# All four groups of a visit gathered and scattered by POOL, without tests of the token count

## The chip, the core and the metric

One core of a Trainium2 chip. The metric is the device time of one execution in microseconds (us). The kernel before takes 1515.26 us, the median of three runs (1512.69 to 1515.73). The core has TensorE (PE in the profile, its weight loads PEld), VectorE (DVE), ScalarE (ACT), GpSimd (POOL) and SyncE (SP), and 16 DMA engines that all queues share.

## What is computed

One decoder layer for 512 tokens of width 1024, in float32: a gated DeltaNet group and a convolution group side by side, one output projection, and then a mixture of experts. The last part is where the change lies. Cut to what matters:

```python
def _moe(xn, w_router, b_router, w_gate_up, b_gate_up, w_down, b_down):
    logits = (xt @ w_router + b_router).astype(jnp.float32)
    top_val, top_idx = lax.top_k(logits, TOP_K)          # 4 of 32 experts for each token
    gates = jax.nn.softmax(top_val, axis=-1)
...
    def expert_block(args):
        x_blk, e = args
        hid = x_blk @ w_gate_up[e] + b_gate_up[e]
        gate, up = hid[:, :D_FF], hid[:, D_FF:]
        gate = jnp.minimum(gate, SWIGLU_LIMIT)
        up = jnp.clip(up, -SWIGLU_LIMIT, SWIGLU_LIMIT)
        glu = gate * jax.nn.sigmoid(SWIGLU_ALPHA * gate)
        return ((up + 1.0) * glu) @ w_down[e] + b_down[e]
...
    y = jax.ops.segment_sum(weighted, row_tok, num_segments=t + 1)[:t]
```

512 tokens with 4 experts each are 2048 pairs over 32 experts, 64 for an expert on average.

## The kernel before

The first 420 us or so compute the two mixing groups, the output projection and the router. Then the kernel goes through the experts one after the other, a **visit** each. With the counts of these inputs there are 32 visits. A visit has room for 128 tokens, in four **groups** of 32 slots (`GROUPS`, `GROUP`). A group's tokens lie on 128 partitions: each token's row of 1024 numbers is cut into four quarters, and each quarter has a partition of its own. So a gather or a scatter of one group handles 128 rows of 256 numbers (1 KB). TensorE skips the matmuls of groups 2 and 3 when the visit has no more than 64 or 96 tokens; groups 0 and 1 are always computed.

DVE works out, from the router's choice, for every slot the row in memory (`idx`). A slot without a token gets a number of 2048 or more, past the bound that both indirect transfers are given (`bounds_check=PAST - 1`), and such a row is skipped.

POOL's part is the loop at L605 that this case is about. It runs 31 times (`m` is 30), once for each visit but the last. Pass `i` has two halves:

- The **gather half** waits until TensorE has turned the tokens of visit `i + 1` (`xt_done`), copies the four index columns of visit `i + 2` (`fetch_rows`, L551), and issues the gathers of that visit into `xg` (a part of `wq`; `gather`, L556). They raise `gathered` by 16 each. TensorE waits for that before it turns these tokens, one pass later (`xt_turn`).
- The **scatter half** waits until ACT has written the results of visit `i - 1` into `yb` (a part of `rows`; `y_ready`), copies the indices (L551 again), and issues the scatters, which add to `acc_dram` in memory (`scatter`, L561). They raise `scattered` by 16 each. POOL then waits until all scatters so far have landed and raises `landed`. ACT waits for `landed` before it writes the next visit's results over `yb`, and POOL itself can't begin the next gather half before.

Groups 0 and 1 are issued always. For groups 2 and 3 the helper `full_or_idle` reads the visit's token count from `left` into a register and branches: a group with tokens gets its gather or scatter, one without gets `idle` (L568), a transfer of 16 bytes from `gdn_dt_bias` into the tile `spare`, so that the semaphore rises by 16 all the same. The three visits whose gathers stand ahead of the loop (12 gathers), and the last visit's scatters behind it (4), have no test: all four groups are issued there.

The other queues around it: SP issues a visit's weights, 8 transfers of 1 MB for gate/up into the eight slots of `ring` (L375) and 4 of 1 MB for down into `dslots` (L380), each when TensorE has used the slot before (`gu_used`, `d_used`). TensorE, in pass `i`, runs the gate/up matmuls of visit `i` (L1869), turns the gathered tokens of visit `i + 1` (L1836), and runs the down matmuls of visit `i - 1` (L1905) with the turning of the hidden values between (L1931). ACT copies the hidden values (L887) and writes the results (L895). DVE applies the biases and the gate (L1431 to L1450). At the end SP waits for `scattered`, loads the sum back (L419), and it is normalised and written out.

Of the kernel before, what the change touches and what calls it, by code (L numbers as in the profile page):

```python
# [32 lines left out]
GROUP = 32  # L33
GROUPS = 4
# [4 lines left out]
def block_kernel(nc, x, attn_norm_w, w_in, gdn_conv_w, gdn_a_log, gdn_dt_bias, gdn_norm_w, cf_dw_w, cf_dw_b,  # L39
# [3 lines left out]
    H = gdn_a_log.shape[1]  # L43
# [27 lines left out]
    with ExitStack() as ctx:  # L71
        def sb(name, cols, dt=F32):
            return ctx.enter_context(nc.sbuf_tensor(name, [P, cols], dt))
# [22 lines left out]
        idx_in, idx_out = sb("idx_in", GROUPS, I32), sb("idx_out", GROUPS, I32)  # L96
        n_iter = sb("n_iter", 1, I32)
        left = sb("left", ROUNDS_MAX * E + 2, I32)
        spare = sb("spare", 4 * H)
        count16 = sb("count16", 2 * P, BF16)  # L100
        tri16, ones16 = count16[:, 0:P], count16[:, P:2 * P]

# [227 lines left out]
        def tokens_left(engine, i):  # L330

            return engine.value_load(left[0:1, bass.ds(i, 1)], min_val=0, max_val=SEQ)
# [94 lines left out]
        def _(pool):  # L427
# [135 lines left out]
                                        in_=yb[:, g, :], in_offset=None, bounds_check=PAST - 1,  # L563
                                        oob_is_err=False, compute_op=ALU.add).then_inc(scattered, 16)

            def idle(k, done):

                pool.dma_start(spare[0:1, k * H:(k + 1) * H], gdn_dt_bias[0:1, :]).then_inc(done, 16)  # L568

            def full_or_idle(i, full, empty):  # L570

                tokens = tokens_left(pool, i)
                with pool.If(tokens > 2 * GROUP):
                    full(2)
                    with pool.If(tokens > 3 * GROUP):
                        full(3)
                    with pool.Else():
                        empty(3)
                with pool.Else():
                    empty(2)  # L580
                    empty(3)

            pool.wait_ge(idx_ready, 1)
            fetch_rows(idx_in, 0, 1)
            for g in range(GROUPS):
# [19 lines left out]
            with pool.Fori(1, m + 2) as i:  # L605
                pool.wait_ge(idx_ready, i + 3)
                pool.wait_ge(xt_done, i + 2)
                pool.sem_inc(pool_step, 1)
                fetch_rows(idx_in, (i + 2) % STAGES, i * 2 + 2)
                for g in range(2):  # L610
                    gather(g)
                full_or_idle(i + 2, gather, lambda g: idle(g - 2, gathered))
                pool.wait_ge(y_ready, i + 1)
                pool.sem_inc(pool_step, 1)
                fetch_rows(idx_out, (i - 1) % STAGES, i * 2 + 3)
                for g in range(2):
                    scatter(g)
                full_or_idle(i - 1, scatter, lambda g: idle(g, scattered))
                pool.wait_ge(scattered, i * (16 * GROUPS))
                pool.sem_inc(landed, 1)  # L620
            pool.wait_ge(y_ready, m + 3)
# [1365 lines left out]
```

## Time and profile before

| | |
|---|---|
| median of three runs | 1515.26 us |
| the profiled execution | 1512.43 us |
| its span, first to last instruction | 1510.7 us |
| TensorE busy | 1369.0 us (91%) |
| DVE, ACT, POOL busy | 565.8, 301.8, 368.6 us (37, 20, 24%) |
| DMA | 451.10 MB, mean 299 GB/s; about 400 in the expert stage |
| weights of the experts | 256 + 124 + 4 transfers of 1 MB |
| POOL's loop: gathers, scatters, small transfers | 88, 83, 93 |

How to read it: the busy times are of one profiled execution, so everything that is added up from the trace is held against 1512.43 us; the difference to the 1510.7 us of the span lies outside the first and last instruction. Two engines or an engine and the DMA can be busy at once, so the busy times say only who has room. Who is waited for is told by the views of waits, which name for each idle time what ended it, and by the timeline, which gives an engine's instructions one by one with the idle time before each.

### The profile page before, as it was taken

The page shows a single profiled execution, that of the slowest core. Times are in us where ns is not written, and L with a number is a line of the kernel's source. Part 1 is how long each engine was busy: PE and PEld are TensorE (multiplying, and loading weights), DVE is VectorE, ACT ScalarE, POOL GpSimd, SP SyncE. Part 2 cuts the span into 40 slices and gives each one's busy share as a digit, 9 for nine tenths or more (in the row PEclk, how much of TensorE's full clock was granted, in tenths as well). Part 3 has the DMA queues.
Part 4 walks back from the last instruction along what each step waited for, and adds up shares of the span by engine and source line. Part 5 has one row for each costly group of instructions (what it writes and reads, how often), then busy time and mean ns, then how long its engine had stood idle before and what let it go on. Part 6 is the DMA issues. An engine that isn't in the chain of part 4 may idle for free.

```text
span 1510.7 us, 33686 instructions
## 1 busy us (share of the span) xinstructions
PE 1369.0 (91%) x13162; PEld 633.5 (42%) x13163; DVE 565.8 (37%) x1174; ACT 301.8 (20%) x566; POOL 368.6 (24%) x434
## 2 busy tenths in 40 slices
PE   6997989879899999999999999988988988889982
PEld 3444555555433444343433444433433433334441
DVE  2888888553522223322232212332222223222231
ACT  3122323131301212121211112211111111112122
POOL 4001111010221232331342223232223223222323
PEclk9999999979969999999999999999999999999996
DMA  9211000300387999999999999999999999999974
GB/s 301 79 66 56 1 29 1 148 21 18 125 312 298 375 382 388 399 410 406 408 399 409 405 410 409 405 408 401 401 410 403 407 405 399 399 404 406 401 302 139
DMA packets 109974, 451.10 MB, mean 299 GB/s; under 512 B 18264, under 2 KB 36852, under 8 KB 77142
## 3 DMA queue, kind: packets, MB, share of 16 engines
q1 hardware_dynamic: 86566, 427.88, 70.8%
q0 software_dynamic: 20304, 21.03, 6.1%
q10 hardware_dynamic: 3072, 1.76, 0.5%
q8 instruction: 21, 0.34, 0.1%
q14 instruction: 11, 0.09, 0.0%
HBM read 439.05 MB, written 17.17 MB: 302 GB/s over the span
## 4 chain that ended last, share of the span: by engine, by line
PE 61%; DMA 20%; DVE 10%; SPq 4%; ACT 2%; issue 2%; POOL 0%; ACTq 0%; DVEq 0%; POOLq 0%
PE bank L1869 28%; DMA ring<-in_w_gate_up_dram 19%; PE bank L1905 12%; PE bank L1552 5%; PE bank L1719 4%; PE bank L1931 3%; DVE dslots L1007 2%; SPq L380 2%; SPq L375 2%; PE bank L1836 1%; DVE qkbuf L1031 1%; PE bank L1854 1%; PE bank L1618 1%; PE bank L1547 1%; PE bank L1825 1%
## 5 line engine op out<-in xcount | busy, mean ns | idle before, releaser
L1869 PE MATMUL bank<-ring,wq 128*32 128x512 f32 x5184 | 590.0, 608 | 49.3 <-DMA ring<-in_w_gate_up_dram 46.4
L1869 PEld LDWEIGHTS bank<-ring,wq 128*32 128x32 f32 x5184 | 163.7, 112 | 425.2 <-issue 424.5
L1905 PE MATMUL bank<-dslots,intra 128*32 128x256 f32 x5056 | 286.0, 380 | 0.0
L1905 PEld LDWEIGHTS bank<-dslots,intra 128*32 128x32 f32 x5056 | 157.8, 110 | 108.6 <-issue 11.1
L887 ACT ACTIVATE wq<-bank 128x512 f32<-128x512 f32 x128 | 66.1, 602 | 632.3 <-PE bank L1869 632.3
L561 POOL DMA_INDIRECT acc_rows<-rows,idx_out x83 | 151.0, 1819 | 46.2 <-POOL idx_out L551 28.3
L1431 DVE TENSOR_TENSOR intra<-bank,small 128x256 f32<-128x256 f32 x128 | 45.4, 417 | 293.1 <-PE bank L1931 293.1
L1552 PE MATMUL bank<-hbuf,ring 128*128 128x512 f32 x320 | 147.7, 603 | 0.0
L1360 DVE TENSOR_REDUCE small<-bank 128x4 f32<-128x8 f32 x34 | 5.7, 167 | 343.9 <-PE bank L1825 343.9
L551 POOL COPY idx_in<-idx 128x4 int32 (+1 forms) x34 | 6.3, 186 | 456.9 <-PE bank L1836 405.7
L556 POOL DMA_INDIRECT wq<-xn_rows,idx_in x88 | 91.9, 1044 | 49.7 <-POOL idx_in L551 29.3
L1007 DVE SCALAR_TENSOR_TENSOR dslots<-dslots,small 128x512 f32<-128x512 f32 x120 | 91.8, 765 | 2.7
L1438 DVE TENSOR_TENSOR zrows<-bank,small 128x256 f32<-128x256 f32 x128 | 45.4, 417 | 101.7 <-PE bank L1931 101.7
L1552 PEld LDWEIGHTS bank<-hbuf,ring 128*128 128x128 f32 x320 | 58.7, 194 | 58.4 <-issue 58.4
L1931 PE MATMUL bank<-consts,wq 128*128 128x128 f32 x512 | 70.8, 282 | 2.7 <-DVEq L1434 1.6
L901 ACT ACTIVATE zrows<-intra 128x1024 f32<-128x1024 f32 x32 | 33.8, 1057 | 185.0 <-DVE intra L1435 185.0
L568 POOL DMA_DIRECT2D spare<-in_gdn_dt_bias_dram x93 | 69.3, 848 | 0.1
L1931 PEld LDWEIGHTS bank<-consts,wq 128*128 128x128 f32 x512 | 55.7, 142 | 28.7 <-issue 25.5
L1719 PE MATMUL bank<-ring,dslots 128*128 128x512 f32 x128 | 59.6, 611 | 1.9 <-DVE dslots L1186 1.9
L895 ACT ACTIVATE rows<-bank,small 128x256 f32<-128x256 f32 x128 | 50.2, 475 | 51.6 <-PE bank L1905 51.6
L551 POOL COPY idx_out<-idx 128x4 int32 (+1 forms) x32 | 6.8, 214 | 210.1 <-ACT rows L895 210.1
L1339 DVE TENSOR_SCALAR rows<-slot_no,small 128x512 bf16<-128x512 bf16 x140 | 40.1, 351 | 10.5 <-DVE idx L1363 10.3
(267 smaller groups left out, 1040.6 us busy)
## 6 DMA issues: line engine op xcount, KB each, us to landing
ring<-in_w_gate_up_dram SPq DMA_DIRECT2D x256, 1024.0 KB, 21.3
dslots<-in_w_down_dram SPq DMA_DIRECT2D x124, 1024.0 KB, 24.5
ring<-in_w_in_dram SPq DMA_DIRECT2D x12, 1024.0 KB, 12.1
ring<-in_w_out_dram SPq DMA_DIRECT2D x4, 1024.0 KB, 4.8
ring<-in_w_down_dram SPq DMA_DIRECT2D x4, 1024.0 KB, 20.5
rows<-in_x_dram SPq DMA_DIRECT2D x4, 512.0 KB, 6.6
hbuf<-in_x_dram SPq DMA_DIRECT2D x4, 512.0 KB, 4.6
xn_rows<-convbuf POOLq DMA_DIRECT2D x4, 512.0 KB, 4.2
```

The source lines that it names most:

```text
L556: pool.indirect_dma_start(out=xg[:, g, :], out_offset=None, in_=xn_q, in_offset=bass.IndirectOffsetOnAxis(ap=idx_in[:, g:g + 1], axis=0), ...
L561: pool.indirect_dma_start(out=acc_q, out_offset=bass.IndirectOffsetOnAxis(ap=idx_out[:, g:g + 1], axis=0), in_=yb[:, g, :], in_offset=None ...
L568: pool.dma_start(spare[0:1, k * H:(k + 1) * H], gdn_dt_bias[0:1, :]).then_inc(done, 16)
L887: A(hid[:, g, :], bank[g][:, :], ACT.Copy).then_inc(hid_ready, 1)
L895: ins = A(yb[:, g, :], bank[4 + g // 2][:, (g % 2) * QD:(g % 2 + 1) * QD], ACT.Copy, scale=gates[:, bass.ds(stage * GROUPS + g, 1)])
L1007: own.mark(V.scalar_tensor_tensor(out=cacc[:, j, :], in0=ubuf[:, j, k:k + SEQ], scalar=PT[:, j, k:k + 1], in1=cacc[:, j, :], op0=ALU.mult, ...
L1431: V.tensor_tensor(four(g2[:, g, :, :]), four(src[g]), bias(0), ALU.add).then_inc(s, 1)
L1552: ins = M(bank_of(s)[:, :], unit_ap(u)[:, c, half * P:(half + 1) * P], hT[:, c, :], start=(c == 0), stop=(c == KC - 1))
L1719: ins = M(pair[half][:, :], lhs, w, start=(kc == 0), stop=(kc == KC - 1))
L1869: ins = M(bank[g][GROUP * j:GROUP * (j + 1), :], xT[:, g, c % 2, (c // 2) * GROUP:(c // 2 + 1) * GROUP], w[:, :, j * QD:(j + 1) * QD], sta ...
L1905: ins = M(b[GROUP * j:GROUP * (j + 1), col:col + QD], actT[:, g, c % 2, (c // 2) * GROUP:(c // 2 + 1) * GROUP], w[:, cc, j * QD:(j + 1) * QD],
L1931: ins = TR(bank[6 + g // 2][:, c:c + P], hid[:, g, half * QD + hh * P:half * QD + (hh + 1) * P], ident)
```

## The change

In the loop of POOL, groups 2 and 3 get their gather and their scatter in every pass, like groups 0 and 1. The helpers `idle` and `full_or_idle` go, with the reading of the token count on POOL, its branches, and the tile `spare`. The counts that everyone waits for stay the same, since a gather or scatter raises its semaphore by 16 as the small transfer did. Nothing changes on the other engines: TensorE still tests the count and skips its matmuls.

```diff
--- before.py
+++ after.py
@@ -96,7 +96,6 @@
         idx_in, idx_out = sb("idx_in", GROUPS, I32), sb("idx_out", GROUPS, I32)
         n_iter = sb("n_iter", 1, I32)
         left = sb("left", ROUNDS_MAX * E + 2, I32)
-        spare = sb("spare", 4 * H)
         count16 = sb("count16", 2 * P, BF16)
         tri16, ones16 = count16[:, 0:P], count16[:, P:2 * P]
 
@@ -563,23 +562,6 @@
                                         in_=yb[:, g, :], in_offset=None, bounds_check=PAST - 1,
                                         oob_is_err=False, compute_op=ALU.add).then_inc(scattered, 16)
 
-            def idle(k, done):
-
-                pool.dma_start(spare[0:1, k * H:(k + 1) * H], gdn_dt_bias[0:1, :]).then_inc(done, 16)
-
-            def full_or_idle(i, full, empty):
-
-                tokens = tokens_left(pool, i)
-                with pool.If(tokens > 2 * GROUP):
-                    full(2)
-                    with pool.If(tokens > 3 * GROUP):
-                        full(3)
-                    with pool.Else():
-                        empty(3)
-                with pool.Else():
-                    empty(2)
-                    empty(3)
-
             pool.wait_ge(idx_ready, 1)
             fetch_rows(idx_in, 0, 1)
             for g in range(GROUPS):
@@ -607,15 +589,13 @@
                 pool.wait_ge(xt_done, i + 2)
                 pool.sem_inc(pool_step, 1)
                 fetch_rows(idx_in, (i + 2) % STAGES, i * 2 + 2)
-                for g in range(2):
+                for g in range(GROUPS):
                     gather(g)
-                full_or_idle(i + 2, gather, lambda g: idle(g - 2, gathered))
                 pool.wait_ge(y_ready, i + 1)
                 pool.sem_inc(pool_step, 1)
                 fetch_rows(idx_out, (i - 1) % STAGES, i * 2 + 3)
-                for g in range(2):
+                for g in range(GROUPS):
                     scatter(g)
-                full_or_idle(i - 1, scatter, lambda g: idle(g, scattered))
                 pool.wait_ge(scattered, i * (16 * GROUPS))
                 pool.sem_inc(landed, 1)
             pool.wait_ge(y_ready, m + 3)
```

The order in which POOL's instructions stand shows it at two places. First the gather half of the loop. Before (`wq` holds the gathered tokens, `xn_rows` is the memory they come from, `left` the token counts):

```order
L556 DMA wq<-xn_rows,idx_in 128x256 [waits rows_known]
L556 DMA wq<-xn_rows,idx_in 128x256
L332 ISA
L332 TENSOR_LOAD left
L332 ISA x2
L573 COMPARE_AND_BRANCH
L556 DMA wq<-xn_rows,idx_in 128x256
L575 COMPARE_AND_BRANCH
L556 DMA wq<-xn_rows,idx_in 128x256
L575 UNCONDITIONAL_BRANCH
L568 DMA spare<-in_gdn_dt_bias_dram 1x4x1
L577 UNCONDITIONAL_BRANCH
```

After the change, from behind the index copy on:

```order
L551 ISA
L555 DMA wq<-xn_rows,idx_in 128x256 [waits rows_known]
L555 DMA wq<-xn_rows,idx_in 128x256 x3
L594 REGISTER_ALU
L550 ISA [waits y_ready]
L550 COPY idx_out<-idx 128x4
L551 REGISTER_ALU
```

The load of the count, its branches and the small transfers are gone, and four gathers stand together; the wait on `y_ready` follows them directly.

Second the scatter half, from behind the first two scatters. Before (`acc_rows` is the sum in memory, `idx_out` the rows to add to):

```order
L573 COMPARE_AND_BRANCH
L561 DMA acc_rows<-rows,idx_out 2048x256
L575 COMPARE_AND_BRANCH
L561 DMA acc_rows<-rows,idx_out 2048x256
L575 UNCONDITIONAL_BRANCH
L568 DMA spare<-in_gdn_dt_bias_dram 1x4x1
L577 UNCONDITIONAL_BRANCH
L568 DMA spare<-in_gdn_dt_bias_dram 1x4x1 x2
L579 UNCONDITIONAL_BRANCH
L619 REGISTER_ALU
L605 ISA [waits scattered]
```

After the change, the four scatters and the wait behind them:

```order
L560 DMA acc_rows<-rows,idx_out 2048x256 [waits rows_known]
L560 DMA acc_rows<-rows,idx_out 2048x256 x3
L599 REGISTER_ALU
L587 ISA [waits scattered]
L587 COMPARE_AND_BRANCH
```

The wait on `scattered` now stands behind four scatters in every pass, where it stood behind two, three or four of them and small transfers.

## Rows read from the trace of the kernel before

**Rows 1.** Busy times of the engines in the stretch 505 to 1400 us.

```profile
core 0: us, PE busy (x) PEld busy (x) DVE busy (x) ACT busy (x) POOL busy (x), PEclk, DMA share, GB/s
505.00:1400.00 895.00, 849.16 (x10004) 362.69 (x9996) 234.35 (x554) 156.23 (x304) 261.69 (x280) 0.98 1.02 402
```

**Rows 2.** Waits of TensorE, 500 to 1400 us: us in total, times, longest.

```profile
PE bank L1869 <- DMA ring<-in_w_gate_up_dram: 45.2, 28, 3.3
```

**Rows 3.** The chain that ended last, 500 to 1400 us, by line.

```profile
by line: PE bank L1869 39.9%; DMA ring<-in_w_gate_up_dram 29.5%; PE bank L1905 17.1%; PE bank L1931 3.4%; SPq L380 3.3%; SPq L375 2.9%; PE bank L1836 1.9%; PE bank L1825 0.9%; issue 0.9%; SPq L404 0.0%; SPq L402 0.0%; SPq L407 0.0%
```

**Rows 4.** Waits of POOL, whole program, those for its own transfers.

```profile
POOL idx_in L551 <- DMA spare<-in_gdn_dt_bias_dram: 18.3, 2, 9.9
...
POOL idx_in L551 <- DMA acc_rows<-rows,idx_out: 17.1, 2, 10.1
```

**Rows 5.** Groups (busy us, mean ns | idle), then issues with us to landing.

```profile
L561 POOL DMA_INDIRECT acc_rows<-rows,idx_out x83 | 151.0, 1819 | 46.2 <-POOL idx_out L551 28.3
...
L556 POOL DMA_INDIRECT wq<-xn_rows,idx_in x88 | 91.9, 1044 | 49.7 <-POOL idx_in L551 29.3
...
L568 POOL DMA_DIRECT2D spare<-in_gdn_dt_bias_dram x93 | 69.3, 848 | 0.1
...
wq<-xn_rows,idx_in POOLq DMA_INDIRECT x88, 6.1
acc_rows<-rows,idx_out POOLq DMA_INDIRECT x83, 8.4
```

**Rows 6.** DMA queue 0 in 1494:1495.3 (packets, MB, share); slices of 1490:1495.3.

```profile
q0 software_dynamic: 144, 0.00, 5.5%
...
DMA  8510000823532200000002300000000000022000
```

**Rows 7.** Timeline of POOL, the end: start us, us, what, idle before.

```profile
1473.11 1.67 POOL L561 DMA_INDIRECT acc_rows<-rows,idx_out  x1 [2.41 <-issue]
...
1476.95 1.56 POOL L561 DMA_INDIRECT acc_rows<-rows,idx_out  x1 [0.30 <-issue]
...
1492.55 1.55 POOL L561 DMA_INDIRECT acc_rows<-rows,idx_out  x1 [0.30 <-issue]
```

**Rows 8.** Timeline of POOL, a light visit.

```profile
914.95 0.19 POOL L551 COPY idx_in<-idx 128x4 int32 x1 [20.79 <-PE bank L1836]
916.07 1.09 POOL L556 DMA_INDIRECT wq<-xn_rows,idx_in  x1 [0.93 <-POOL idx_in L551]
917.47 1.03 POOL L556 DMA_INDIRECT wq<-xn_rows,idx_in  x1 [0.30 <-issue]
918.50 1.10 POOL L568 DMA_DIRECT2D spare<-in_gdn_dt_bias_dram  x2
924.96 0.19 POOL L551 COPY idx_out<-idx 128x4 int32 x1 [5.35 <-ACT rows L895]
...
939.95 0.19 POOL L551 COPY idx_in<-idx 128x4 int32 x1 [8.63 <-PE bank L1836]
```

**Rows 9.** Timeline of POOL, a visit with both upper groups real.

```profile
956.61 0.19 POOL L551 COPY idx_out<-idx 128x4 int32 x1 [11.87 <-ACT rows L895]
...
975.72 0.19 POOL L551 COPY idx_in<-idx 128x4 int32 x1 [10.15 <-DMA acc_rows<-rows,idx_out]
```

**Rows 10.** Timeline of DVE and of ACT, single rows.

```profile
1471.74 1.22 DVE L1445 TENSOR_TENSOR intra<-intra,zrows 128x1024 f32<-128x1024 f32 x1
...
979.48 1.57 ACT L895 ACTIVATE rows<-bank,small 128x256 f32<-128x256 f32 x4 [0.26 <-PE bank L1905]
...
1484.10 0.47 ACT L895 ACTIVATE rows<-bank,small 128x256 f32<-128x256 f32 x1 [13.89 <-PE bank L1905]
```

**Rows 11.** DMA queues, 1427 to 1442 us: packets, MB, share of 16 engines.

```profile
q1 hardware_dynamic: 962, 6.23, 100.7%
q0 software_dynamic: 160, 0.00, 0.7%
```

**Rows 12.** Line 561 between 1473 and 1478.4 us: its three scatters' landing.

```profile
DMA to landing us min/median/max: 3.1/4.0/4.5
```

## The prediction

> **What bounds the kernel now.** The expert stage fills the program from about 500 us on, so I read its busy times first: between 505 and 1400 us TensorE is busy for 849 of 895 us, POOL for 262, and the DMA engines' share is 1.02 at 402 GB/s [rows 1]. The waits say what TensorE's other 46 us are: 45.2 us in 28 pieces for the gate/up weights, and no row for a gather, for ACT or for DVE [rows 2]. In the chain of work that ended last, from 500 to 1400 us, stand TensorE's lines and the weight DMA with 29.5%, and no line of POOL [rows 3]. So a visit costs what its matmuls or its 12 MB of weights cost, whichever is later. POOL matters in three ways only: if it comes so late that ACT or TensorE must wait for it, if its transfers take DMA time from the weights, and at the end, where its last scatters are on the chain. POOL idles for 895 - 262 = 633 us in this stretch, 21 us a visit; only four times in the program does it wait for its own earlier transfers to land (18.3 and 17.1 us) [rows 4].
>
> **The counts.** The trace has 88 gathers, 83 scatters and 93 small transfers [rows 5]. The loop runs 31 times; 12 gathers stand ahead of it and 4 scatters behind. Its gathers are thus 62 unconditional and 14 conditional, its scatters 62 and 17, and the small transfers 62 - 14 = 48 and 62 - 17 = 45, together 93. After the change these 93 are gone, and 48 gathers and 45 scatters are added (136 and 128 in all). Every added one belongs to a group without a token, so it moves no row.
>
> **What an empty group costs POOL.** The last scatter of the program is such a one: its DMA is 144 packets with 0.00 MB [rows 6], and it held POOL for 1.55 us, as long as the scatter at 1476.95 [rows 7]. The duration does not hang on the rows moved. A gather takes 1.03 us and has a gap of 0.30 us before it; a scatter 1.55 and 0.30; two small transfers 1.10 together, so 0.55 each, without a gap [rows 7, 8]. Added are 48 x (1.33 - 0.55) = 37 us and 45 x (1.85 - 0.55) = 58 us of POOL, 95 in all or 3.1 us a visit. What goes besides, two register loads and the branches, leaves no idle time before the small transfer at 918.50 [rows 8]: zero here; if it is worth something, the 3.1 us are less. All of it lies beside POOL's 21 idle us a visit, unless a single visit is too tight.
>
> **The tight visits.** A visit in which both upper groups were real is the template. From its copy of the scatter indices at 956.61 us to the next copy of gather indices, released by the landing of the fourth scatter at 975.72, it took 19.1 us [rows 9]. In a light visit the copy was at 924.96 and the next one, released by TensorE, at 939.95, 15.0 us later [rows 8]. So with four scatters POOL is late there by 19.1 - 15.0 = 4.1 us at most, and by nothing at least, if empty scatters land as soon as the real ones before them. Then four gathers: 1.1 (copy to first gather) + 3 x 1.33 + 1.0 = 6.1 us, so the gather half ends by 939.95 + 4.1 + 6.1 = 950.2, and POOL's next input comes at 956.61 anyway. The lateness is gone within the visit. Who waits for POOL meanwhile? ACT's results need the earlier scatter landed: in this visit they are wanted about 1.9 us before the copy, 954.7, and POOL gives the word at 944.1. TensorE's next turn of gathered tokens comes before 975.72, at about 970; gathers issued by 949 land 6.1 us later [rows 5], 955. The tightest place I see is behind the full visit itself: landed at 975.72, ACT's next results at 979.48 [rows 9, 10], 3.8 us of cover, with TensorE, not POOL, as what they waited for. A light visit after the change is no heavier than this one. Cost on the path: 0, under a cover of 3.8 us or more.
>
> The added instructions may take longer than these durations. At 1473.11 a scatter came 2.41 us after the index copy, with DVE's 1.22 us operation of 1471.74 just ended [rows 7, 10], and the mean of all scatters is 1.82 us against 1.55 [rows 5]. By these rows the added ones would cost 0.3 us more each, and where such a gap falls 1.5 us more; 0 on the path again, inside the 3.8 us. The Trainium skill, "SBUF — State Buffer", SBUF: two separate sides, has a rule that speaks against the change: while DVE runs an operation in its two-port mode, GpSimd is locked out and cannot write DMA descriptors. By that rule the 2.41 us gap is such a lock and every added indirect transfer is one more that can meet it; the sum stays what it is, since the whole gap is within the cover.
>
> **DMA time.** This is the one term that I do not set to zero. The empty scatter's 144 packets take 5.5% of 16 engines in a window of 1.3 us, 0.072 us of the whole DMA side [rows 6]. Two empty gathers and two small transfers together are 160 packets and 0.7% of 15 us, 0.105 us, or 0.66 ns a packet [rows 11]. An estimate: 16 packets of each transfer are its completions, so a small transfer has 32 packets and an empty gather 48. Added are then 45 x 0.072 = 3.2 us and 48 x 48 x 0.66 ns = 1.5 us, removed 93 x 32 x 0.66 ns = 2.0 us: net 2.8 us (unrounded). This is the upper end, if all of it delays weights; the lower end is 0, if such packets pass where others leave room. The weight DMA is on the chain for 29.5% of the time [rows 3], so I take 0.3 x 2.8 = 0.8 us.
>
> **The end.** The loop's last scatter half has three scatters and a small transfer; its fourth scatter would start at 1476.95 + 1.85 = 1478.8 [rows 7]. The three others land in at most 4.5 us there [rows 12], so it lands by 1483.3. ACT's last results, which need it, begin at 1484.10, when TensorE's last matmul is done [rows 10]. Cost 0, with 0.8 us to spare; were it to take the 8.4 us median of all scatters [rows 5], 3.1 us. The four scatters behind the loop stay.
>
> Sum: 1512.43 us (the profiled execution; its span is 1510.7) + 0.8 = 1513.2. The median of the runs shown is 1515.26, 2.8 us above that execution, so I state 1516.
>
> **Rivals.**
> *Slower: the empty rows hold the DMA engines.* The share counts only the time that packets take. In the 40 slices of 1490 to 1495.3 us (0.13 us each) the last scatter is the pair of 2s near the end [rows 6]: its packets pass within 0.27 us. If the engines moved no weights in that time, an empty scatter would cost 0.27, a gather 48/144 of it, 0.09, and a small transfer 32/144, 0.06: 45 x 0.27 + 48 x 0.09 - 93 x 0.06 = 10.9 us, 1526. Its place is the gate/up weights in flight after each scatter, and it decides the sign once over a quarter of the price is real (3 of 10.9). Against it: around the two empty gathers the weight queue keeps 100.7% [rows 11]. Chance 0.13. The Trainium skill, "DMA: Bandwidth & Descriptors", Latency and other measured facts, offers as a best guess a mechanism of this sort: the engines fetch GpSimd's descriptors from SBUF, and two of the sixteen are slowed by it. No row here tells the engines apart.
> *Slower at the end:* the fourth scatter of the last loop pass misses 1484.10. Price 3.1 us, 1519; it decides only when the DMA term is at its upper end too. Chance 0.05.
> *Faster:* the small transfers were a burden that the shares hide, and empty groups pass for nothing. At 0.06 us each 93 x 0.06 = 5.6 us go: 1510. For it: two of POOL's waits for its own transfers end on a small one [rows 4]. Against: TensorE waits for weights alone [rows 2]. Chance 0.10.
> *The change does not do what it says* (other counts than 136 and 128): the time would be near 1515. Chance 0.01.
>
> **Chances.** The forecast has 0.71, with a range of its own of 1512 to 1518. A measurement of this kernel can tell about 0.2%, 3 us, from no change. Faster by more: 0.10 and a tail of the forecast, 0.11. Slower by more: 0.13, half of the end's 0.05 and a tail, 0.16. Same: 0.73. The range takes in the better part of the faster case and the lower half of the DMA case: 1511 to 1521.
>
> **What would show it.** Right: 136 gathers of about 1.0 us, 128 scatters of 1.5 to 2.1; POOL's busy time up by some 48 x 1.03 + 45 x 1.55 - 93 x 0.55 = 68 us; more of its gather halves released by a scatter's landing, none over 4.1 us later than TensorE's turn; and TensorE's waits in the stage still near 45 us, for weights alone. Wrong: a wait of TensorE or ACT for a gather or scatter; TensorE's waits for gate/up weights well above 45 us with the weights landing later; or ACT's last results starting after TensorE's last matmul.

## The result, and the profile after

| | before | after |
|---|---|---|
| median of five runs | 1515.26 us (1512.69 to 1515.73) | 1525.35 us (1522.04 to 1527.23) |
| ratio after to before, 95% interval | | 1.0065 (1.0046 to 1.0084) |
| the profiled execution; its span | 1512.43; 1510.7 us | 1524.62; 1522.8 us |

The changed kernel is slower by 0.65%, about 10 us. The forecast was 1516, next to no change, with a range of 1511 to 1521: the time lies outside it. Three of the five runs behind the 1515.26 us are those shown ahead of the prediction. Two further jobs that ran both kernels gave 1.0093 and 1.0095, a third 1.0040 (see the experiments). The page of the profile after: its busy times, DMA queues and the groups of the down matmuls and of POOL's transfers (line, engine, operation, count, then busy us, mean ns of one, idle time before):

```profile
PE 1396.5 (92%) x13162; PEld 663.0 (44%) x13163; DVE 565.7 (37%) x1174; ACT 300.4 (20%) x566; POOL 434.2 (29%) x433
...
q1 hardware_dynamic: 86566, 427.88, 70.6%
q0 software_dynamic: 26112, 21.09, 6.3%
...
L1885 PE MATMUL bank<-dslots,intra 128*32 128x256 f32 x5056 | 323.9, 381 | 7.2 <-issue 0.8
L560 POOL DMA_INDIRECT acc_rows<-rows,idx_out x128 | 216.9, 1694 | 58.0 <-issue 31.5
...
L555 POOL DMA_INDIRECT wq<-xn_rows,idx_in x136 | 141.1, 1037 | 62.9 <-issue 32.3
```

The counts are 136 and 128, the small transfers are gone, and POOL is busy for 434.2 us instead of 368.6: as forecast. What was not forecast is TensorE's part. It is busy for 1396.5 us instead of 1369.0, though it has the same work. The down matmuls (L1905 before, L1885 after) have grown by more than that. Before, their group read so:

```profile
L1905 PE MATMUL bank<-dslots,intra 128*32 128x256 f32 x5056 | 286.0, 380 | 0.0
```

The same 5056 matmuls, each as long as before (380 and 381 ns; they overlap), take 37.9 us more of the engine, and 7.2 us of idle time has come between them. The stage between 505 and 1400 us, and TensorE's waits between 500 and 1400, which answer [rows 1, 2]:

```profile
505.00:1400.00 895.00, 865.03 (x9896) 387.53 (x9892) 233.79 (x551) 152.06 (x297) 315.41 (x274) 0.99 1.02 398
```

```profile
PE bank L1849 <- DMA ring<-in_w_gate_up_dram: 22.9, 16, 2.1
PE bank L1849 <- issue: 1.3, 2, 0.7
```

TensorE is busy for 865 us where it was busy for 849, and waits for weights half as long. The chain from 500 to 1400 us answers [rows 3]:

```profile
by line: PE bank L1849 47.3%; PE bank L1885 25.1%; DMA ring<-in_w_gate_up_dram 14.1%; PE bank L1911 4.9%; PE bank L1816 2.5%; SPq L374 1.9%; SPq L379 1.9%; PE bank L1805 1.2%; issue 1.1%; SPq L403 0.0%; SPq L401 0.0%; SPq L406 0.0%
```

The weight DMA's part has fallen from 29.5% to 14.1%. No line of POOL stands there. So this profile says that TensorE itself has become slower in one place. The timeline of one light pass shows how. PE, then PEld, of after (start, us, what, idle time before), with POOL's instructions behind them:

```profile
928.50 1.09 PE L1911 MATMUL bank<-consts,wq 128*128 128x128 f32 x8
929.52 4.52 PE L1885 MATMUL bank<-dslots,intra 128*32 128x256 f32 x64
```

```profile
929.52 1.88 PEld L1885 LDWEIGHTS bank<-dslots,intra 128*32 128x32 f32 x40 [0.17 <-issue]
931.79 0.16 PEld L1885 LDWEIGHTS bank<-dslots,intra 128*32 128x32 f32 x5 [0.39 <-issue]
932.54 1.02 PEld L1885 LDWEIGHTS bank<-dslots,intra 128*32 128x32 f32 x19 [0.58 <-issue]
```

```profile
929.63 1.00 POOL L555 DMA_INDIRECT wq<-xn_rows,idx_in  x1 [0.31 <-issue]
930.93 1.27 POOL L555 DMA_INDIRECT wq<-xn_rows,idx_in  x1 [0.30 <-issue]
```

The 64 matmuls take 4.52 us, where the 64 ahead of them (at 924.91) take 3.66. Within them the weight loads stop twice, for 0.39 and 0.58 us, released by nothing that the trace shows ("issue" means that the engine waits for nothing the profile shows; whether it lacks instructions or is held some other way, no row tells). The stops lie beside POOL's third and fourth gather. I call such a place a **patch**. By the same timeline there is one in 27 of the 31 passes. Against the same number of matmuls in a profile without them, a pass loses 0.4 to 2.5 us in its down block (mostly 1.4 to 2.4), idle time included, and all of them together 45 us; in the four others (copies at 627.49, 790.5, 988.87 and 1014.51 us) POOL was late, and its third and fourth gather fell behind the down block.

### The profile page after: what moved, and what is told of

Its sections match the earlier page's. It is cut to its first block, busy times and chain, and to the rows that moved or that the text cites. A ratio compares the mean times of both kernels' runs of the same rounds, so it can differ in the third digit from the quotient of the medians.

```text
span 1522.8 us, 33414 instructions
## 1 busy us (share of the span) xinstructions
PE 1396.5 (92%) x13162; PEld 663.0 (44%) x13163; DVE 565.7 (37%) x1174; ACT 300.4 (20%) x566; POOL 434.2 (29%) x433
## 2 busy tenths in 40 slices
DMA packets 115782, 451.17 MB, mean 296 GB/s; under 512 B 24072, under 2 KB 42660, under 8 KB 82950
## 3 DMA queue, kind: packets, MB, share of 16 engines
q0 software_dynamic: 26112, 21.09, 6.3%
HBM read 445.34 MB, written 23.07 MB: 308 GB/s over the span
## 4 chain that ended last, share of the span: by engine, by line
PE 74%; DVE 10%; DMA 9%; SPq 2%; ACT 2%; issue 2%; POOL 0%; ACTq 0%; DVEq 0%; POOLq 0%
PE bank L1849 33%; PE bank L1885 18%; DMA ring<-in_w_gate_up_dram 8%; PE bank L1532 5%; PE bank L1699 4%; PE bank L1911 4%; DVE dslots L987 2%; PE bank L1816 2%; DVE qkbuf L1011 1%; SPq L374 1%; SPq L379 1%; PE bank L1834 1%; PE bank L1805 1%; PE bank L1598 1%; PE bank L1527 1%
## 5 line engine op out<-in xcount | busy, mean ns | idle before, releaser
L1849 PE MATMUL bank<-ring,wq 128*32 128x512 f32 x5184 | 582.8, 602 | 26.3 <-DMA ring<-in_w_gate_up_dram 22.9
L1849 PEld LDWEIGHTS bank<-ring,wq 128*32 128x32 f32 x5184 | 179.2, 111 | 379.0 <-issue 370.2
L1885 PE MATMUL bank<-dslots,intra 128*32 128x256 f32 x5056 | 323.9, 381 | 7.2 <-issue 0.8
L560 POOL DMA_INDIRECT acc_rows<-rows,idx_out x128 | 216.9, 1694 | 58.0 <-issue 31.5
L1885 PEld LDWEIGHTS bank<-dslots,intra 128*32 128x32 f32 x5056 | 173.1, 109 | 138.1 <-issue 59.6
L555 POOL DMA_INDIRECT wq<-xn_rows,idx_in x136 | 141.1, 1037 | 62.9 <-issue 32.3
L875 ACT ACTIVATE rows<-bank,small 128x256 f32<-128x256 f32 x128 | 49.9, 472 | 66.4 <-PE bank L1885 53.5
L489 POOL TENSOR_TENSOR sqbuf<-qkbuf 128x512 f32<-128x512 f32 x8 | 10.4, 1306 | 126.6 <-DVE qkbuf L1029 126.6
```

Of the source, the lines that this page charges most:

```text
L555: pool.indirect_dma_start(out=xg[:, g, :], out_offset=None, in_=xn_q, in_offset=bass.IndirectOffsetOnAxis(ap=idx_in[:, g:g + 1], axis=0), ...
L560: pool.indirect_dma_start(out=acc_q, out_offset=bass.IndirectOffsetOnAxis(ap=idx_out[:, g:g + 1], axis=0), in_=yb[:, g, :], in_offset=None ...
L875: ins = A(yb[:, g, :], bank[4 + g // 2][:, (g % 2) * QD:(g % 2 + 1) * QD], ACT.Copy, scale=gates[:, bass.ds(stage * GROUPS + g, 1)])
L1849: ins = M(bank[g][GROUP * j:GROUP * (j + 1), :], xT[:, g, c % 2, (c // 2) * GROUP:(c // 2 + 1) * GROUP], w[:, :, j * QD:(j + 1) * QD], sta ...
L1885: ins = M(b[GROUP * j:GROUP * (j + 1), col:col + QD], actT[:, g, c % 2, (c // 2) * GROUP:(c // 2 + 1) * GROUP], w[:, cc, j * QD:(j + 1) * QD],
```

## The experiments

Kernels ran in jobs of one to four, each job on one chip and with its own runs of the kernel before. The ratios below are against those. Whether a kernel shows patches turned out to belong to the job and not to the program.

**Halves and whole, as edits of before.** First theory: the empty groups cost DMA time. Rival: it is the missing tests, small transfers or the place of the code that TensorE feels. The first three kernels keep before's code; both branches do the full transfer, or one half has four transfers.

```diff
-                full_or_idle(i + 2, gather, lambda g: idle(g - 2, gathered))
+                full_or_idle(i + 2, gather, gather)
...
-                full_or_idle(i - 1, scatter, lambda g: idle(g, scattered))
+                full_or_idle(i - 1, scatter, scatter)
```

> The kernel before, with its register load and its branches on POOL, but each branch without tokens issues the gather or scatter in place of the small transfer: the DMA work of the changed kernel (136 gathers, 128 scatters) in the program of the kernel before. Theory A (the added empty gathers and scatters themselves, by their packets or by their timing, starve TensorE in the down matmuls): slow patches in the down matmuls in nearly all visits, TensorE's line of down matmuls busy for about 324 us, and 1525 us, within 2 us of the changed kernel. Theory B (it is POOL's program without tests, its place or its pace, and not the empty groups): no slow patches, 286 us for the down matmuls, and 1513 to 1517 us.

Gathers alone (the scatter half keeps its branches):

```diff
-                for g in range(2):
+                for g in range(GROUPS):
                     gather(g)
-                full_or_idle(i + 2, gather, lambda g: idle(g - 2, gathered))
```

> Only the gather half of the change: four gathers in every pass without a test, the scatter half with its test and its small transfers. The slow patches in the changed kernel begin with the landing of a pass's gathers, so theory A1 (it is the gather half) expects them here in nearly every pass, 324 us for the down matmuls and 1523 to 1526 us. Theory A2 (it is the scatter half: its 45 empty scatters) expects none, and 1514 to 1517. Theory B (any change of POOL's program can bring the patches or not) makes no forecast of which of the two single halves shows them.

Scatters alone is the same edit in the other half.

> Only the scatter half of the change: four scatters in every pass without a test, the gather half with its test and its small transfers. Theory A1 (gather half): no slow patches in the down matmuls, 286 us there, 1513 to 1517 us. Theory A2 (scatter half): slow patches, 324 us, 1523 to 1526. The prediction's rival of DMA packets would give most of its 10.9 us here (45 x 0.27 = 12 us less 45 x 0.06), about 1524, with TensorE waiting longer for gate/up weights and no slow patches.

The fourth is after with the tile `spare` put back, and with 32 instructions behind POOL's program under a condition that can't hold. None of those is in what ran (33414 instructions, as in after), so in effect it is after with one tile more.

```diff
+        spare = sb("spare", 4 * H)
...
+            with pool.If(m > 8 * E):
+                for _ in range(PADDING):
+                    nc.gpsimd.memset(osq[:, 0:1], 0.0)
```

> The changed kernel with the unused tile kept at its old place in SBUF and 32 small instructions added at the very end of POOL's program, in a branch that is never taken: nothing that runs differs from the changed kernel but one compare at the end. Theory A (what is executed decides): slow patches and 1525 us as before, within 2 us. Theory B (the length and place of POOL's program or of a tile decides): it may lose the slow patches and come back to 1513 to 1517 us; if it does, no executed instruction was the cause.

Measured, beside 1512.02 us: both 1.0034 (1.0022 to 1.0046), gathers 1.0009 (0.9997 to 1.0022), scatters 1.0013 (0.9998 to 1.0028), after with the tile 1.0033 (1.0019 to 1.0048). None has patches; the down group of e4 reads:

```profile
L1890 PE MATMUL bank<-dslots,intra 128*32 128x256 f32 x5056 | 286.1, 380 | 0.1
```

So the added transfers cost 0.33% with branches and without them, and the two halves add up to about that within their intervals. The rest of the 0.65% came with the patches. After these four I thought that the tile or the code's place made the patches.

**Tile and place.** After unaltered, after with the tile, and after and before with 25 more instructions on POOL ahead of the loop, on the same chip:

```diff
+            for _ in range(PADDING):
+                own.mark(nc.gpsimd.memset(idx_out[:, :], 0))
+                own.settle()
             with pool.Fori(1, m + 2) as i:
```

> The changed kernel, unaltered, beside kernels that differ from it by a detail. Two kernels with the same empty gathers and scatters came out at 1.0034 and 1.0033 of the kernel before, without slow patches. Theory B1 (the patches belong to this very program): they are here again, TensorE busy some 27 us more than in the kernel before, ratio 1.006 to 1.007. Theory B2 (they belong to that one session, by the memory it was given): no patches, ratio 1.0033, as the two others.

> The changed kernel with the unused tile of 64 bytes a partition kept at its old place, so that the tile behind it lies where it lay before; POOL's program is the changed one. If the patches come from that tile's place: none here, ratio 1.0033. If they come from POOL's shorter program (or its length's effect on where other things lie): patches, 1.006 to 1.007. If from the session alone: none here nor in the unaltered one, 1.0033 in both.

> The changed kernel without the tile, with 25 tiny memsets on POOL just ahead of its loop, where it idles for 24 us: POOL's program has as many instructions as that of the kernel before (180). If the patches come from the shorter program: none here, ratio 1.0033. If from the tile: patches, 1.006 to 1.007. If from the session: none, 1.0033.

> The kernel before with the same 25 memsets ahead of POOL's loop, 205 instructions. POOL idles there, so by what is executed it is worth 0: ratio 1.000 within its interval. If the length of POOL's program can bring slow patches to a program with no empty group, this may show it: patches in the down matmuls and 3 to 5 us more.

Measured, beside 1513.77 us: 1.0093 (1.0067 to 1.0119), 1.0095 (1.0067 to 1.0123), 1.0079 (1.0051 to 1.0107), and before with 25 more 0.9993 (0.9976 to 1.001). The down groups of e6 and e8:

```profile
L1886 PE MATMUL bank<-dslots,intra 128*32 128x256 f32 x5056 | 321.7, 381 | 15.2 <-issue 9.3
```

```profile
L1909 PE MATMUL bank<-dslots,intra 128*32 128x256 f32 x5056 | 301.7, 381 | 3.5 <-issue 1.1
```

Tile and place are out: e6 runs the same instructions as e4, all 13162 matmuls in the same order, and has patches where e4 had none, on the same chip in another job. And the before-type kernel e8 has them too, 16 us of busy time and 3 of idle: in its 2 passes with four gathers 2.0 and 2.8 us over what the same number of matmuls takes without patches, in its 10 with three gathers 1.0 us on average. Of the 19 with two gathers and two small transfers 9 have none and 10 some 0.4 to 0.9 us, 0.3 us on average. So a patch grows with the number of gathers in the pass, and the third and fourth aren't its only condition. (The expectation of e11 names lower figures for e8: 1.75, 0.3 and none. Its trace has these.) One pass with four gathers, TensorE's timeline of e8, then the same pass of before:

```profile
844.77 6.98 PE L1909 MATMUL bank<-dslots,intra 128*32 128x256 f32 x87
852.09 0.82 PE L1909 MATMUL bank<-dslots,intra 128*32 128x256 f32 x9 [0.34 <-issue]
```

```profile
841.00 5.39 PE L1905 MATMUL bank<-dslots,intra 128*32 128x256 f32 x96
```

96 matmuls take 8.1 us with a patch and 5.39 without; POOL gathers four groups in both.

**Repeats on another chip**, to separate kernel from job: the e4, e1 and e2 kernels again, and before itself as one of the four.

> The same kernel as in the fourth run, word for word. Its order of instructions is the same, engine by engine, as that of the sixth (the builder dropped the 32 added instructions, since their condition can never hold), and yet the fourth had no slow patches and 1.0033, the sixth had them and 1.0095. Theory S (the patches come with the session, that is with the memory or the state that all kernels of one job find): the four kernels of this job agree with each other, either all with patches where a pass has three or four gathers, or none. Theory P (they belong to the program): no patches here, 1.003, whatever the others show.

> The same kernel as in the first run: all groups gathered and scattered, with the load and the branches. Then no patches and 1.0034. Theory S: patches and 1.007 to 1.010 if the others of this job have them, else 1.003 again. Theory P: no patches, 1.003.

> The kernel before itself, for its trace in this job; the ratio is 1.000 within its interval. Theory S, in a job with patches: patches only in the passes with three or four gathers (12 of 31), as in the eighth run, where the passes with four had about 1.75 us more in the down matmuls, those with three 0.3 us and those with two none; in a job without, no patches. Theory P: no patches, as in the first trace of this kernel.

> The same kernel as in the second run: four gathers in every pass, the scatters as in the kernel before. Then no patches and 1.0009. Theory S: if this job has patches, they are in nearly all of its passes, since every pass has four gathers, and the ratio is 1.004 to 1.007; if the job has none, 1.001 again. Theory P: no patches, 1.001.

Measured, beside 1510.11 us: 1.0037 (1.0024 to 1.0051), 1.0032 (1.0017 to 1.0047), 1.0000 (0.9989 to 1.0012), 1.0021 (1.0007 to 1.0035). No patches in any.

**After unaltered again, with its look-alike** (the e4 kernel), before with 25 more, and before. If patches belong to the program, after must have them here and the look-alike not.

> The changed kernel, unaltered, a third time. Theory P (the program's layout): slow patches, 1.0065 to 1.0095, though its look-alike beside it has none. Theory S (the job): the same ratio as the look-alike beside it, either 1.003 and no patches in both or 1.007 to 1.010 and patches in both.

> The look-alike with the tile and the dropped branch, which came out at 1.0033 and 1.0037 without patches. Theory P: the same again, 1.003 to 1.004, no patches. Theory S: it agrees with the changed kernel beside it.

> The kernel before with 25 memsets ahead of POOL's loop, which had patches in its passes with three or four gathers in the job in which the changed kernel had them too. Theory P: patches again in those passes, ratio 0.999 to 1.001. Theory S: patches only if the changed kernel beside it has them.

> The kernel before, for its trace in this job. Theory P: no patches, as in both of its traces. Theory S: patches in the 12 passes with three or four gathers if the changed kernel beside it has patches, none otherwise. Ratio 1.000 either way.

Measured, beside 1509.99 us: 1.0040 (1.0025 to 1.0054), 1.0044 (1.0031 to 1.0056), 1.0000 (0.9987 to 1.0013), 1.0004 (0.9991 to 1.0017). The unaltered kernel has no patches here. Its down group, its 64 matmuls of the pass shown above, and its TensorE waits between 500 and 1400 us:

```profile
L1885 PE MATMUL bank<-dslots,intra 128*32 128x256 f32 x5056 | 286.1, 380 | 0.1
```

```profile
920.21 3.66 PE L1885 MATMUL bank<-dslots,intra 128*32 128x256 f32 x64
```

```profile
PE bank L1849 <- DMA ring<-in_w_gate_up_dram: 49.1, 32, 3.4
```

This is the plain cost of the change, without patches: six runs of three kernels that issue every transfer gave 1.0032 to 1.0044, which is 5 to 6.6 us; their intervals reach from 1.0017 to 1.0056. Where it goes is told by TensorE's gate/up group, the matmuls that wait for weights. Before, then f1 (busy us, mean ns, idle before):

```profile
L1869 PE MATMUL bank<-ring,wq 128*32 128x512 f32 x5184 | 590.0, 608 | 49.3 <-DMA ring<-in_w_gate_up_dram 46.4
```

```profile
L1849 PE MATMUL bank<-ring,wq 128*32 128x512 f32 x5184 | 592.2, 609 | 53.6 <-DMA ring<-in_w_gate_up_dram 50.6
```

Neither number alone is steady: in the four profiles of before-type kernels without patches (before, e11, f3, f4) the busy time goes from 586.5 to 593.5 us and the idle time from 53.5 down to 46.0, so that when the matmuls are shorter the waits are longer. Their sum is 638.8 to 640.0 us in all four. In the six profiles with every transfer (e1, e10, e4, e9, f1, f2) it is 640.9 to 645.8, on the mean 643.3 against 639.4, so 3.9 us more. Scatters alone have 641.2, gathers alone twice 641.6, so each half takes about a half. The down group with its idle time adds 0.9 us (286.9 against 286.0). That is 4.8 of the 5.4 us by which the spans of these profiles differ, and it lies where TensorE waits for weights.

What delays the weights is told by the DMA queues. Between 500 and 1400 us (packets, MB, share of 16 engines), before, e3 (scatters), e2 (gathers) and f1 (after), in this order:

```profile
q1 hardware_dynamic: 62007, 347.81, 94.8%
q0 software_dynamic: 16153, 14.37, 7.7%
```

```profile
q1 hardware_dynamic: 61726, 346.87, 94.6%
q0 software_dynamic: 20656, 14.38, 7.9%
```

```profile
q1 hardware_dynamic: 61920, 346.76, 94.8%
q0 software_dynamic: 16865, 14.50, 7.7%
```

```profile
q1 hardware_dynamic: 61741, 345.77, 94.7%
q0 software_dynamic: 21430, 14.44, 8.0%
```

The four of before's kind move 347.69 to 348.06 MB and the six with every transfer 345.51 to 346.23. The means are 347.87 and 345.86, 0.58% less, and 0.58% of 900 us is 5.2 us. That is the same slowdown once more and names no cause by itself: after moves only 343.32 MB, and there TensorE sets most passes. The cause is in the times of the packets. POOL's queue takes 0.3% more, 2.7 us of 900, which is the share-based price of the prediction, and it takes that with the scatters, not with the gathers (7.9 and 7.7%). The rest is in the weights. In the packet records of these traces a weight packet of 8 KB takes 317.3 to 318.3 ns on the mean in the four of before's kind and 318.7 to 319.5 in the six, 0.4% longer, about 3 us of the window. With the gathers alone it is 318.8 and 319.1, with the scatters alone 317.6. So the empty scatters cost the time of their own packets, and the empty gathers, whose own packets hardly show, cost through slower weight packets.

**Is it lateness or DMA?** Last rival for the rest: POOL comes too late for ACT. In f1 no wait of TensorE or ACT ends on one of POOL's gathers or scatters, and its chain from 500 to 1400 us has no line of POOL:

```profile
by line: PE bank L1849 36.8%; DMA ring<-in_w_gate_up_dram 26.4%; PE bank L1885 17.3%; SPq L379 6.1%; SPq L374 6.1%; PE bank L1911 3.0%; PE bank L1816 1.9%; issue 1.4%; PE bank L1805 0.9%; SPq L403 0.1%; SPq L401 0.1%; SPq L406 0.0%
```

So lateness isn't what the plain cost is. How much more of it would be harmless was asked by one more kernel. After with two more scatters a pass, both fully empty (62 in all), beside after itself:

```diff
+            def scatter_none():
+                pool.indirect_dma_start(out=acc_q,
+                                        out_offset=bass.IndirectOffsetOnAxis(ap=idx_none[:, 0:1], axis=0),
...
+                for _ in range(EXTRA):
+                    scatter_none()
-                pool.wait_ge(scattered, i * (16 * GROUPS))
+                pool.wait_ge(scattered, i * (16 * (GROUPS + EXTRA)))
```

> The changed kernel with two more scatters in each of the 31 passes, all of whose 128 rows are skipped (62 more empty scatters, 3.7 us more of POOL a pass). Theory D1 (DMA time by the packets' share, 0.072 us each): 4.5 us more than the changed kernel beside it, weights moved between 500 and 1400 us down from about 345.8 to 344.2 MB. Theory D2 (DMA time by the 0.27 us in which the packets pass): 17 us more, 340 MB. Theory L (what costs is POOL's lateness, landing too late for ACT's results): waits of ACT for POOL or of TensorE for ACT's results appear, and the loss is far from proportional, 20 us or more for a release 3.7 us later in each pass. If neither costs (theory 0): the same time as the changed kernel.

> The changed kernel, as the reference for the run above in the same job. 1.004 of the kernel before without slow patches, or 1.007 to 1.010 with them; the kernel above then has them too (theory S), and the difference between the two is read either way.

Measured, beside 1515.06 us: 1.0101 (1.0084 to 1.0117) and after 1.0095 (1.0078 to 1.0112). Patches in both. The waits of POOL and of ACT in g1 (us in all, times, longest):

```profile
POOL idx_in L552 <- DMA acc_rows<-rows,idx_none: 229.2, 23, 13.2
```

```profile
ACT rows L887 <- POOLq L612: 27.2, 7, 6.7
```

Here POOL does come late: in 23 passes it waits for its own scatters, and ACT waits for it 7 times, up to 6.7 us. Between 584 and 677 us the chain that ended last runs through POOL: its scatters, the landing of the added ones in three passes and at last that of a gather. The landings are 13.75, 13.11 and 12.82 us of it. The chain of the whole execution by line:

```profile
PE bank L1861 27%; PE bank L1897 15%; DMA ring<-in_w_gate_up_dram 11%; PE bank L1544 5%; PE bank L1711 4%; PE bank L1923 3%; DMA acc_rows<-rows,idx_none 3%; DVE dslots L999 2%; SPq L381 2%; SPq L376 2%; PE bank L1828 2%; DVE qkbuf L1023 1%; POOL acc_rows L562 1%; PE bank L1846 1%; PE bank L1610 1%
```

The time still grows by only 1.5 us, within the intervals, but two changes offset each other in it. The gate/up group with its idle time takes 618.6 us in g1 and 606.3 in g2, 12.3 more; the down group takes 326.2 and 336.9, 10.7 less, since with POOL late the gathers fell behind the down block more often: g1 has nine passes without a patch there, g2 four. So the run doesn't show that lateness of this size is harmless, and it settles neither that nor the price of an empty scatter (62 of them would be 4.5 us at 0.072 us each and 17 at 0.27). A repeat in a job without patches would have; none was made.

A kernel without small transfers and without empty groups was not tried, so what a small transfer costs by itself isn't known.

## Why the prediction was wrong

**What bounds the kernel** stood. Without patches it is the same picture: f1's waits in the stage are for gate/up weights alone (but for 0.3 us), its TensorE is busy for 845.3 us where before was for 849.2. The sign that I had named for a wrong DMA term, waits well above 45 us, is hardly there (49.1, and 49.0 in f4, which has no added transfer). The waits alone can't show it: they move against the matmuls' busy time by up to 7 us from run to run, and a fixed window holds fewer matmuls of a longer stage. Busy and idle time of the gate/up group over the whole program do show it (643.3 us against 639.4).

**The counts and POOL's cost** were right: 5808 more packets (26112 - 20304; the estimate of 16 completion packets for a transfer gives 45 x 144 + 48 x 48 - 93 x 32 = 5808), and 65.6 us more of POOL where 68 was forecast.

**The tight visits** were right in what they concluded. POOL waits for the landing of scatters 6 times in f1 and 11 times in after, where it did 2 times [rows 4]. The row of f1, then that of after:

```profile
POOL idx_in L550 <- DMA acc_rows<-rows,idx_out: 52.3, 6, 10.7
```

```profile
POOL idx_in L550 <- DMA acc_rows<-rows,idx_out: 103.6, 11, 10.6
```

No wait of TensorE or ACT ends on it in f1 or in after. Whether the cover is the 3.8 us that I named wasn't measured; in g1, with 3.7 us more of POOL a pass, it was passed and POOL stood on the chain.

**The DVE gap** was sized as "0.3 us more each", and 1.5 where a gap falls. The 45 added scatters brought 71.2 us of busy time in f1, 1.58 each, the 48 gathers 49.7 us, 1.04 each, and the idle time before both kinds grew from 95.9 to 120.9 us, 0.27 for each added one: as long as undisturbed ones, with the usual gap. By the rule of the Trainium skill ("SBUF — State Buffer", SBUF: two separate sides) DVE can lock GpSimd out. It isn't what cost the time here, since the added transfers met no gap longer than the usual 0.30 us on average.

**DMA time: the step that failed.** The term stands as 0.3 x 2.8 = 0.8 us. Measured is 5 to 6.6 us without patches. Two things in it are wrong. The factor 0.3 is the share of the chain that stands under the weight DMA's name; but the gate/up blocks became 3.9 us longer and the down blocks 0.9, so the whole delay and more than it came through, not three tenths of it. And the 2.8 us, called the upper end, counted the time of the empty packets only. The 0.4% by which weight packets take longer is another 3 us, and the sum of the two is near the measured value. The rival "the empty rows hold the DMA engines" named the place and the sign. Its price of 10.9 us was twice too high, and it put nearly all of it on the scatters, which have about half; its point of decision, 3 us, was passed. Row 11's "the weight queue keeps 100.7%" was my evidence against it. That is a share of busy time, which stays full when the same MB take longer, so it could not speak against it. What the Trainium skill offers there as a best guess ("DMA: Bandwidth & Descriptors", Latency and other measured facts), that GpSimd's descriptors slow two of the sixteen engines, would fit the slower weight packets; no row here tells engines apart, so it stays open.

**The end** was right: in after the fourth scatter of the last loop pass was issued at 1489.29, and ACT's last results began at 1496.49, released by TensorE; in f1 the two are 1485.58 and 1491.84. Timelines of POOL and ACT in after:

```profile
1489.29 1.54 POOL L560 DMA_INDIRECT acc_rows<-rows,idx_out  x1 [0.31 <-issue]
```

```profile
1496.49 0.47 ACT L875 ACTIVATE rows<-bank,small 128x256 f32<-128x256 f32 x1 [14.89 <-PE bank L1885]
```

**The patches were in no rival.** The sum put TensorE's own work at its old length, and that failed too. They add what lies between 1.0040 (f1) and 1.0065 to 1.0095 (after in three jobs), so 4 to 8 us, and put the result outside the range. The cost is smaller than the 45 us (37.9 busy, 7.2 idle) by which the down blocks of after are longer, since most of that is taken from the gate/up blocks: 609.1 us with their waits in after, 643.3 on the mean without patches. The weights are there sooner (22.9 us of waits in the stage, 49.1 in f1), and the gate/up matmuls themselves take 582.8 us where they took 590.0, at a mean granted clock of 0.965 of full speed against 0.958. The change doesn't make the patches, which e8 shows in a before-type kernel; it raises the passes with a third or fourth gather from 12 to 31, and the patches are longest there. With only 12, before loses less: its median is 1513.77 to 1515.26 us in the three jobs with patches and 1509.99 to 1512.02 us in the three without, which fits but isn't shown by a profile of before itself, since the one with rows ahead of the prediction has none.

What holds TensorE beside POOL's gathers, and what in a job brings it about, stays open. The trace shows no transfer that TensorE waits for; the packets of the instruction queues are the same in after, f1 and before (21 and 11); and tile, length and place of code don't decide it. The share, count and length of the gathers are alike in f1 and after.

## What to carry to other kernels

An indirect DMA whose rows are all out of bounds moves no data, but its packets still pass the DMA engines. Where the DMA is the bound, let the whole delay through to the time, and take the share that the queues' row shows for a lower bound: here the cost was about twice that. Read it from busy and idle time together of the matmuls that the transfers feed, and from what a packet of the other queue takes, not from a share or from waits alone. Ask of every row "from which it could be seen otherwise": a busy share of 100% says nothing about speed. When a run with more of the suspected thing costs nothing, look at its chain before you call the thing harmless. And before a difference of some tenths of a per cent is put down to an edit, run the kernel in more than one job beside a look-alike, and compare the groups of work that both have.

## What was not expected of the hardware

- 93 empty transfers in place of 93 small ones of 16 bytes cost 5 to 6.6 us, 0.05 to 0.07 us each, though they move nothing. The scatters cost through their own packets, the gathers through weight packets that take 0.4% longer.
- In three of the six jobs TensorE stood without anything to wait for beside POOL's third and fourth gather, for 0.39 and 0.58 us in the pass shown, and the same 5056 matmuls took 316 to 324 us of it instead of 286 (302 in a before-type kernel). On one chip both kinds of job occurred.
- In the same jobs ACT and DVE were held as well. In passes without a patch, where POOL's gathers came behind the down block, ACT's results in after began only at 995.91 us, four microseconds after TensorE's down block, and DVE's next operation with them, 0.9 us after the fourth gather had ended at 994.99 (at 634.62 us it is again 0.9). The trace names no local releaser ("remote"); ACT has 3 or 4 such waits in the profiles of after with patches (12.8, 11.0 and 13.7 us in after, e5 and g2) and none in those without. TensorE itself stood there too, 0.67 us ahead of its gate/up block at 993.65 (0.59 at 632.98). TensorE, POOL, ACT and DVE of after:

```profile
993.65 6.93 PE L1849 MATMUL bank<-ring,wq 128*32 128x512 f32 x58 [0.67 <-issue]
993.99 1.00 POOL L555 DMA_INDIRECT wq<-xn_rows,idx_in  x1 [0.30 <-issue]
995.91 1.56 ACT L875 ACTIVATE rows<-bank,small 128x256 f32<-128x256 f32 x4 [3.98 <-remote]
995.94 1.42 DVE L1418 TENSOR_TENSOR zrows<-bank,small 128x256 f32<-128x256 f32 x4 [5.10 <-remote]
```

So it isn't TensorE alone that is held beside these gathers. The delay of ACT and DVE costs nothing here, because TensorE doesn't wait for either.
- The page's count of memory traffic takes the skipped rows as moved: 439.05 MB read before and 445.34 after, 48 x 128 KB more, while the queues' rows have 451.10 and 451.17 MB in all.
